# Value products of heads 4 to 7 in the second attention moved one unit sooner

## What is computed

```python
def mla_kv(z_kv, g_ckv, w_ukv, cos, sin):
    b, n, _ = z_kv.shape
    kv = (rmsnorm(z_kv[..., :KV_LORA], g_ckv) @ w_ukv).reshape(b, n, MLA_HEADS, MLA_NOPE + MLA_V)
    ...
    return k, kv[..., MLA_NOPE:]

def block_attention(q, k, v, scale):
    ...
    def one_block(q_blk):
        s = jnp.einsum('bqgrd,bkgd->bgrqk', q_blk, k, preferred_element_type=jnp.float32) * scale
        p = jax.nn.softmax(s, axis=-1).astype(v.dtype)
        return jnp.einsum('bgrqk,bkgd->bqgrd', p, v)
```

## Time and profile before

| | us |
|---|---|
| median of 3 runs | 1686.37 |
| lowest and highest | 1684.05 and 1687.76 |
| the profiled execution | 1689.88 |
| its span in the trace | 1688.1 |
| mean granted TensorE clock | 0.996 |

### The profile page before, as it was taken

The page is one execution under the profiler, slowest core; times in us unless marked ns, Lnnn a source line. Parts: engine busy times, 40 slices in busy tenths (PEclk is TensorE's granted clock), DMA queues, the critical chain, the costliest instruction groups (busy, mean ns, idle before and its releaser), DMA issues.

```text
span 1688.1 us, 25937 instructions
## 1 busy us (share of the span) xinstructions
PE 1643.1 (97%) x9738; PEld 1476.9 (87%) x9738; DVE 1343.6 (80%) x2261; ACT 825.4 (49%) x1501; POOL 196.6 (12%) x201
## 2 busy tenths in 40 slices
PE   6999999999999999999999999999999999999998
PEld 4788889888999999998888888889888889999876
DVE  5676777767888999997896888969776799998554
ACT  4343266634435555554243534454455566666442
POOL 1068520000300000000000300011210200000000
PEclk9999999999999999999999999999999999999999
DMA  9633130051322444448664122200103123222331
GB/s 354 196 138 109 42 27 1 1 214 61 125 113 107 158 169 164 173 166 328 209 217 159 57 99 77 75 1 1 51 26 113 51 79 120 104 101 101 137 112 64
DMA packets 46059, 194.10 MB, mean 115 GB/s; under 512 B 13040, under 2 KB 13552, under 8 KB 31216
## 3 DMA queue, kind: packets, MB, share of 16 engines
q1 hardware_dynamic: 37248, 187.46, 31.3%
q10 hardware_dynamic: 8688, 4.99, 1.1%
HBM read 180.48 MB, written 11.96 MB: 114 GB/s over the span
## 4 chain that ended last, share of the span: by engine, by line
PE 45%; DVE 4%; ACT 3%; DVEq 1%; issue 1%; ACTq 0%; another core or an unknown queue 0%; POOL 0%
PE PS L1187 6%; PE PS L1193 6%; PE PS L1190 6%; PE PS L820 4%; PE PS L822 4%; PE PS L821 4%; PE PS L1607 2%; PE PS L326 2%; PE PS L334 2%; PE PS L330 2%; PE PS L1591 1%; PE PS L362 1%; PE PS L361 1%; PE PS L358 1%; DVE cat_od L2624 1%
## 5 line engine op out<-in xcount | busy, mean ns | idle before, releaser
L1187 PE MATMUL PS<-w_hi,a_ring 128*128 128x512 f32 x662 | 259.5, 392 | 2.0 <-DVE a_ring L1268 0.9
L1190 PE MATMUL PS<-w_lo,a_ring 128*128 128x512 f32 x662 | 257.8, 389 | 0.0
L315 DVE TENSOR_TENSOR w_lo<-w_raw,w_hi 128x2048 fp32r<-128x2048 f32 x62 | 144.5, 2330 | 101.5 <-ACT w_hi L309 96.9
L309 ACT ACTIVATE w_hi<-w_raw 128x2048 fp32r<-128x2048 f32 x62 | 118.7, 1914 | 161.5 <-PE PS L1187 102.8
L820 PE MATMUL PS<-TH_ff,FH_ff 128*128 128x256 f32 (+1 forms) x608 | 187.4, 308 | 4.1 <-ACT u_ff L836 3.1
L822 PE MATMUL PS<-TH_ff,FL_ff 128*128 128x256 f32 (+1 forms) x608 | 187.3, 308 | 0.0
L821 PE MATMUL PS<-TL_ff,FH_ff 128*128 128x256 f32 (+1 forms) x608 | 187.2, 308 | 0.0
L1187 PEld LDWEIGHTS PS<-w_hi,a_ring 128*128 128x128 f32 x662 | 124.3, 188 | 30.4 <-issue 1.8
L1190 PEld LDWEIGHTS PS<-w_lo,a_ring 128*128 128x128 f32 x662 | 124.4, 188 | 25.1
L820 PE MATMUL PS<-HT,FH_ff 128*128 128x256 f32 (+1 forms) x456 | 140.6, 308 | 0.0
L821 PE MATMUL PS<-HT,FH_ff 128*128 128x256 f32 (+1 forms) x456 | 140.5, 308 | 0.0
(11 more groups left out here) (375 smaller groups left out, 4208.2 us busy)
## 6 DMA issues: line engine op xcount, KB each, us to landing
w_raw<-wpack SPq DMA_DIRECT2D x102, 1024.0 KB, 4.9
m_raw<-modu SPq DMA_DIRECT2D x80, 512.0 KB, 5.8
mod_raw<-modw SPq DMA_DIRECT2D x8, 1024.0 KB, 11.9
a_kept<-yb SPq DMA_DIRECT2D x17, 384.0 KB, 2.3
c_rows<-c_scratch SPq DMA_DIRECT2D x8, 512.0 KB, 5.1
x_kept<-X SPq DMA_DIRECT2D x1, 3072.0 KB, 9.6
A_ff<-a_kept SPq DMA_DIRECT2D x2, 1536.0 KB, 9.1
X<-x_kept SPq DMA_DIRECT2D x1, 3072.0 KB, 10.1
```

The lines of the kernel that those rows point to most:

```text
L309: nc.scalar.activation(w_hi[r][:, :], w_raw[r][:, :], ACT.Copy).then_inc(wh_ready, 1)
L315: nc.vector.tensor_tensor(w_lo[r][:, :], w_raw[r][:, :], w_hi[r][:, :].bitcast(F32), ALU.subtract).then_inc(wl_ready, 1)
L1187: mm = nc.tensor.matmul(o, ah, w_hi[n % 2][:, wc], start=k == 0, stop=False)
L1190: mm = nc.tensor.matmul(o, ah, w_lo[n % 2][:, wc], start=False, stop=False)
```

## The change

The six value pieces come one unit sooner; the keys stay where they are. On PE, `values(0, (3, 4, 5))` is followed by piece 0, and `extra(u)` makes piece u+1 for u = 0 to 4, no piece for u = 5 and 6, and the keys from u = 7 as before. Piece 0 waits for three copied tiles (`odk v` at least 3), since tile 2 used bank 6. On ACT, the copy of value piece u stands at the end of unit u, where it stood at the end of unit u+1. No instruction is added or dropped on any engine; DVE, POOL and the transfers are as before.

```diff
@@ ACT, beside_units
-                if u - 1 in PIECES:
-                    h, part = PIECES[u - 1]
+                piece = u if u < NT else u - 1
+                if u != NT and piece in PIECES:
+                    h, part = PIECES[piece]
                     act.wait_ge(S("odk", "pmm"), piece_of(h, part) + 1)
@@ PE
-            def beside_units(u):
+            def piece(u):
 
                 if u in PIECES:
                     h, part = PIECES[u]
                     i, n = piece_of(h, part), UKV0 + 1
                     if i == 0:
                         weights(pe, n)
+                        pe.wait_ge(S("odk", "v"), 3)
                     else:
                         pe.wait_ge(S("odk", "piece"), i)
...
+            def first_units():
+                values(0, (3, 4, 5))
+                piece(0)
+
+            def beside_units(u):
+
+                if u < NT - 1:
+                    piece(u + 1)
+                elif u >= NT:
+                    piece(u)
                 if u == CLN:
...
-            attn_pe(pe, "od", True, units(True), lambda: values(0, (3, 4, 5)), beside_units, begin_odo)
+            attn_pe(pe, "od", True, units(True), first_units, beside_units, begin_odo)
```

## The result

| kernel | median us | lowest to highest | runs |
|---|---|---|---|
| before, run beside it | 1686.43 | 1684.05 to 1689.12 | 8 |
| changed | 1691.03 | 1689.98 to 1693.18 | 8 |

The ratio is 1.0022 (95%: 1.0014 to 1.0031). The changed kernel is slower by 0.2%: 3.7 us by this ratio, 4.6 by the two medians, "about 4 us" in what follows. That is little, but none of these eight runs of the changed kernel is as fast as the slowest of the eight of before. The forecast was 1686.8 with a range up to 1688.8: the time lies outside, on the side that I had given 0.06. The profiled execution of the changed kernel took 1690.72 us and is close to its median.

A forecast was written before the change was run, and what follows sets the result against it. PE was taken to bound units 1 to 5 and DVE from about unit 8. With signals in time, 0.73 + 0.72 - 1.07 = +0.38 us on 1686.37 gave 1686.8 us, range 1683.2 to 1688.8.

The forecast's parts named there:

- What bounds the kernel: PE sets the pace in units 1 to 5, DVE from about 8; late signals and slow clock cost the profile 4.18 us.
- signals in time: Case where PE's signals come with its matmuls ahead of unit 0: the change costs +0.38 us in sum.
- Piece 0 ahead of unit 0: Six matmuls before unit 0's transposes: +0.73 us with timely signals, 0 with late ones; bounds 0 and 1.47.
- Late case: PE's signals late ahead of unit 0 as in the trace: piece 0 fits the idle time and costs 0.
- rival D: Ahead of unit 0, PE doesn't start piece 0 in the idle time: +0.24, slow clock stays, 1685.5 us; chance 0.14.
- The wait for the copy of piece 0: Behind unit 0's products, PE waits for ACT's copy before piece 1: +0.72 us, bounds 0 and 0.72.
- The return: Unit 5 without a piece: products and DVE's output copy of unit 8 come 1.07 us sooner; bounds 0.66 and 1.40.
- Rival B: DVE decides the end of units 5 to 8 and gives nothing back: slower, 1687.8 us; chance 0.13.
- The sum: Whole stage: +0.38 us with timely signals; with late ones -1.93, or -1.07 if the slow clock stays.
- Which of the two holds in the timed runs?: Around unit 0, most timed runs were taken to have neither late signals nor slow clock; the profile was 3.51 above median.
- Rival C: Late signals near unit 0 are in the earlier timed runs and go away: 1682.6 us; chance 0.08.
- the rule on the clock: Long idle gaps of PE halve the clock; filling the gap ahead of unit 0 would be worth 0.86 with late signals.

The follow-up runs named there:

- undisturbed pair: Kernel before and changed kernel, both with ACT's two gate-row writes moved some 250 us earlier, into the first layer's output stage: 1698.62 and 1699.65 us.
- mid pair: Kernel before and changed kernel, both with the gate-row writes issued behind the second keys' copy, at about 1094: 1689.60 and 1687.35 us.
- before again: The kernel before, nothing changed, run once more for a second profile: 1686.69 us.
- b_sooner: Kernel before with the gate-row writes issued some 8 us sooner, ahead of the four keys' copies: 1687.25 us, ratio 1.0004 to before.
- front_only: Kernel before with only piece 0 moved ahead of unit 0, other pieces and all copies in their old places: 1689.78 us, ratio 1.0010.
- a_copyfirst: Changed kernel with ACT's copy of piece 0 ahead of the rounding, writes where they were: 1690.85 us, ratio 1.0015 to before.
- a_behind: Changed kernel with piece 0 behind the transposes of unit 0 and the scores of unit 2: 1687.62 us, ratio 0.9996 to before.
- a_mid: Changed kernel with the gate-row writes issued behind the second keys' copy, at 1094.1: 1687.35 us, ratio 0.9996 to before.
- changed again: The changed kernel, nothing altered, run once more for a second profile: 1693.05 us.
- b_mid: Kernel before with the gate-row writes issued behind the second keys' copy, at 1094.2: 1689.60 us, ratio 1.0014 to before.
- a_sooner: Changed kernel with the gate-row writes issued some 8 us sooner, ahead of the four keys' copies: 1687.34 us, ratio 1.0004 to before.
- b_early: Kernel before with the gate-row writes moved some 250 us earlier, into the first layer's output stage: 1698.62 us, ratio 1.0062 to before.

## Why the prediction was wrong

By its own steps.

**What bounds the kernel.** Right as far as this: with the signals in time PE idles 0.78 us ahead of the transposes (0.74 forecast), and the first profile's wait and slow clock ahead of and in unit 0 are not in the second.

**Piece 0 ahead of unit 0, +0.73.** Mis-sized by 0.20: 0.93 in the undisturbed pair, since PE idles 0.26 ahead of the piece. Late case: forecast 0, bounds up to 0.24; measured 0.31 in the mid pair, by the holding of PE that stood as rival D.

**The wait for the copy of piece 0, +0.72.** It is there; 0.53 in the undisturbed pair. In the changed kernel itself it isn't seen: by the time PE comes to piece 1 (1118.73), ACT is done with the copy (1117.99 + 0.59).

**The return, -1.07.** Right in all: 1.07 in the undisturbed pair, 1.09 between the profiles shown, 1.08 in the mid pair. Rival B had nothing to it; DVE follows, and is as busy behind as in the earlier trace rows (28.20 of 30 us from 1156 on):

```profile
1156.00:1186.00 30.00, 29.77 (x215) 27.30 (x214) 28.20 (x56) 13.88 (x30) 4.76 (x7) 1.00 0.01 2
```

**The sum.** +0.38 forecast for signals in time, +0.40 measured at C31 of the undisturbed pair. -1.93 for late signals with the clock kept up, -1.80 measured in the mid pair, 2.25 in the timed runs.

**"Which of the two holds in the timed runs?"** This is the step that failed. From the profiled execution's 3.51 us over the median I took it that most timed runs of before have neither late signals nor slow clock. For the slow clock in unit 0 the second profile bears that out. For the late signals it does not: they are there a few us later, where only DVE's maximum of unit 2 meets them and the stage loses 0.65 us. (One trace shows this; that the other runs are like it rests on their times.) I took a disturbance that was missing from the median to be missing from the kernel, and so the sum for "signals in time" has no term for what the later transposes run into: it was put at nothing. In truth the held signals come out 17.5 to 18.2 us behind ACT's two writes in ten of the eleven traces that have the writes near this stage, and 0.93 us of delay was enough to push the transposes' signal into the held stretch: 2.5 to 2.7 us of idle PE ahead of the products of unit 0, and half clock behind. That term is what the changed kernel's two profiles lose over before again at C31, 5.02 and 3.34 us, less the forecast's 0.38.

Rival C had the mechanism by its other end ("frees them or shifts them") but counted only the gain. A rival on the slower side, "the piece shifts a signal that is now in time into the late stretch", had a price in the rows: about the 4.18 us that I had worked out for the wait and the clock together, which gives 1686.37 + 4.18 + 0.38 = 1690.9, against the 1691.03 measured. So close a match would have been luck: the stage lost 5.02 us in one profile and 3.34 in the other.

Of the rule on the clock that was weighed: by the Trainium skill, "TensorE: Matmul & The Clock Gate", section "Why this matters for your kernels", an idle gap that is long enough drops the clock, and is to be avoided in mid-kernel. The mid pair agrees: 0.59 behind 2.57 us of idle PE, 1.00 behind 1.42. In the changed kernel it cuts the other way: the filled gap was followed by a new one, with the slow clock behind that. But the length of the gap alone does not decide: around 213, where the earlier trace rows has 1.00, PE was idle for 3.21 us and the clock stayed up; before again idles 3.19 us in the same place and has half clock behind it.

**What stays open.** What in the writes holds PE's signals, and why to 18 us after them. A hint is in the DMA view: the 2080 packets of the changed kernel's writes are moved by 1100, yet the second write is noted as landed only 19.0 us after its issue at 1097.8, 1.5 us behind the end of the held stretch, and the first one of b_sooner 17.6 us after its own at 1089.9, 0.2 us ahead of it (in the mid pair the first landed within 9 us, the second after 18.8 and 18.4). So PE's signals and the landing of a write come late together; that one waits for the other is not shown. Open too is why the first profile of before had its signals out at 1111.28, only 13.9 us behind the writes at 1097.4, and why the changed kernel should lose more than front_only and a_copyfirst. No kernel tried here beats before by more than the measurement can tell: a_behind and a_mid come nearest, at 0.9996 with intervals from 0.9987 to 1.0005.

## What to carry to other kernels

A wait that no instruction explains ("remote") is a thing with a place of its own in time: find what it follows, here two DMA writes of many small packets, and ask of each change what it moves *into* that stretch, not only what it fills. If a profiled execution is slower than the median by as much as one such wait costs, take a second profile before reasoning from the first: here it showed the same stretch a few us later, one unit off the critical path. And where six matmuls would go in front of a step whose signal others wait for, putting them just behind it keeps that signal in its time: that version of the change was no slower than before, and no faster.

## What the runs showed of the hardware

Behind the two writes of gate rows (2080 packets, issued from ACT's queue), ACT and DVE got signals of PE late: ahead of unit 0 and in it, the waits that ended with the held stretch were 2.6 to 4.6 us, 1.48 for the piece of a_behind. All that is held comes out together, 17.7 (before again), 18.0 (changed), 17.8 (changed again), 17.9 (front_only), 18.2 (a_behind), 17.6 (a_copyfirst), 17.8 (b_mid), 17.9 (a_mid), 17.8 (b_sooner) and 17.5 us (a_sooner) after the issue; the first profile of before, with 13.9, is the exception. With the writes of before 3.9 us sooner (1098.1 to 1094.2) it ended 3.8 us sooner (1115.80 to 1112.01), with them 8.2 us sooner (1089.9) 8.1 us sooner (1107.70), and moving them 250 us away took it out of this stretch: that the writes cause it is shown, how is not. Signals of transposes that started 12.6 us behind the issue got out, those that started 13.5 to 13.6 behind did not. PE itself went on with the scores meanwhile (changed kernel, 1111.44 to 1113.4), but in a_mid it stood for 1.42 us ahead of a piece whose copy was long done.

Loads issued behind the same writes landed late: with the writes at 848, one of `w_raw` 21.5 us and five of `m_raw` 18.8 us (median) after their issue (b_early, 840 to 860), against 7.3 and 4.5 without the writes there (before again).

The half clock in unit 0 followed idle times of PE of 2.3 to 3.35 us (first profile of before, changed, changed again, front_only, a_copyfirst, b_mid), and did not follow 1.42 us (a_mid) or 1.82 us (b_sooner). But 3.21 us around 213 left the clock at 1.00 in the first profile of before, and 3.19 us in the same place of before again did not. In unit 0 the changed kernel's first profile has about twice as long a stretch of it behind 2.71 us of idle time (clock 0.50 from 1117 to 1120 and 0.62 to 1123) as the second has behind 2.49 us (0.81 from 1116 to 1119, 0.62 to 1122); why is open.
